# A hybrid decoder layer: the scaling of the attention probabilities goes from VectorE to GpSimd, GpSimd's scalings get a second scalar, and the stores of the normed rows change queues

## What is computed

```python
h = rms_norm(x, norm_attn)
o_sb  = stick_breaking_attend(q, k, v)          # 8 heads of 64
# NSA: 8 query heads of 64 over 2 kv groups, three branches, mixed by sigmoid gates
p   = softmax(s_branch)                         # branch = compressed, selected, window
o_nsa = gates[0]*(p_cmp@v_cmp) + gates[1]*(p_sel@v_sel) + gates[2]*(p_win@v_win)
x = x + concat(rms_norm(o_sb), rms_norm(o_nsa)) @ w_out
h2 = rms_norm(x, norm_ffn)                      # the "normed rows"
# router: top-1 of 4 groups, top-2 of 4 experts in it; gated MLP of the chosen experts
x = x + hier_moe(h2);  y = rms_norm(x, norm_final)
```

## Time and profile before

| | before |
|---|---|
| runs, median (lowest to highest) | 805.37 us (804.71 to 805.73) |
| the profiled execution's own time | 809.19 us |
| its span, first to last instruction | 807.3 us |
| TensorE busy | 734.5 us (91%) |
| VectorE busy | 374.0 us (46%) |
| ScalarE busy | 219.6 us (27%) |
| GpSimd busy | 105.5 us (13%) |
| mean granted TensorE clock | 0.953 |

### The profile page before, as it was taken

The page is one execution under the profiler, slowest core; times in us unless marked ns, Lnnn a source line. Parts: engine busy times, 40 slices in busy tenths (PEclk is TensorE's granted clock), DMA queues, the critical chain, the costliest instruction groups (busy, mean ns, idle before and its releaser), DMA issues.

```text
span 807.3 us, 12441 instructions
## 1 busy us (share of the span) xinstructions
PE 734.5 (91%) x4713; PEld 396.8 (49%) x4713; DVE 374.0 (46%) x804; ACT 219.6 (27%) x561; POOL 105.5 (13%) x111
## 2 busy tenths in 40 slices
PE   4987899997999698999989986789999999999987
PEld 2554456443645454545555553355555554454532
DVE  5521103376130647695995956364144332323146
ACT  1211111020221364667767731001111101110113
POOL 0121000120000470220210211200000000000050
PEclk9999899999999668999999998789999999999999
DMA  9135881647433970000000255889899999999992
GB/s 332 32 94 167 238 312 41 206 124 234 164 130 109 285 288 1 2 3 1 1 28 1 105 180 213 265 269 318 297 400 410 407 405 398 408 401 400 409 384 109
DMA packets 99422, 172.98 MB, mean 214 GB/s; under 512 B 21314, under 2 KB 38562, under 8 KB 99330
## 3 DMA queue, kind: packets, MB, share of 16 engines
q1 hardware_dynamic: 87986, 150.76, 52.7%
q10 hardware_dynamic: 8112, 11.24, 3.8%
q0 software_dynamic: 3264, 10.17, 3.5%
HBM read 152.95 MB, written 21.28 MB: 216 GB/s over the span
## 4 chain that ended last, share of the span: by engine, by line
PE 53%; DVE 9%; issue 5%; ACT 4%; DMA 4%; POOL 0%; ACTq 0%; DVEq 0%; SPq 0%
PE bank L2417 18%; PE bank L2850 5%; PE bank L1820 5%; PE bank L2408 4%; PE bank L2451 4%; PE bank L2832 4%; PE bank L1766 2%; PE bank L1747 2%; PE bank L2541 1%; PE bank L2536 1%; DVE st L1409 1%; DMA work<-h_rows,ids 1%; PE bank L2400 1%; PE bank L2464 1%; PE bank L1658 1%
## 5 line engine op out<-in xcount | busy, mean ns | idle before, releaser
L2850 PE MATMUL bank<-reg 128*128 128x512 f32 (+1 forms) x384 | 168.1, 585 | 1.2 <-DVE reg L2791 0.9
L2417 PE MATMUL bank<-reg,qreg 128*32 128x128 f32 (+2 forms) x848 | 130.4, 389 | 0.8 <-issue 0.8
L2850 PEld LDWEIGHTS bank<-reg 128*128 128x128 f32 x384 | 72.6, 198 | 70.3 <-issue 67.5
L2417 PEld LDWEIGHTS bank<-reg,qreg 128*32 128x32 f32 (+2 forms) x848 | 66.8, 139 | 59.5 <-issue 48.2
L2832 PE MATMUL bank<-cf,reg 128*128 128x128 f32 (+1 forms) x384 | 63.2, 285 | 18.6 <-DVE reg L2782 9.5
L1820 PE MATMUL bank<-reg 128*128 128x512 f32 x128 | 63.8, 622 | 0.4 <-DVE x L1527 0.3
L2832 PEld LDWEIGHTS bank<-cf,reg 128*128 128x128 f32 (+1 forms) x384 | 43.4, 146 | 36.7 <-issue 30.5
L2707 ACT ACTIVATE work<-bank 128x128 f32<-128x128 f32 (+6 forms) x107 | 40.8, 412 | 44.8 <-PE bank L2832 43.9
L2791 DVE COPY work<-bank 128x128 f32<-128x128 f32 (+4 forms) x56 | 23.2, 428 | 54.1 <-PE bank L2832 54.0
L1249 ACT ACTIVATE reg<-bank,st 128x128 f32<-128x128 f32 (+3 forms) x64 | 33.1, 524 | 40.7 <-DVE st L1409 40.6
L1766 PE MATMUL bank<-work,vreg 128*64 128x128 f32 x480 | 38.5, 291 | 2.1 <-DVE work L2791 1.8
(11 more groups left out here) (340 smaller groups left out, 940.1 us busy)
## 6 DMA issues: line engine op xcount, KB each, us to landing
reg<-w_gate SPq DMA_DIRECT2D x12, 2048.0 KB, 20.3
reg<-w_up SPq DMA_DIRECT2D x12, 2048.0 KB, 22.5
reg<-w_down SPq DMA_DIRECT2D x12, 2048.0 KB, 20.2
reg<-w_in SPq DMA_DIRECT2D x16, 512.0 KB, 6.0
expert_rows<-vreg SPq DMA_DIRECT2D x11, 512.0 KB, 5.3
reg<-cache_sb_k SPq DMA_DIRECT2D x16, 256.0 KB, 4.6
reg<-cache_sb_v SPq DMA_DIRECT2D x16, 256.0 KB, 4.8
qreg<-w_up SPq DMA_DIRECT2D x2, 2048.0 KB, 15.9
```

What stands on the lines that cost most here:

```text
L2417: ins = T.matmul(bank[which][rows, at_:at_ + w], rowsT[b][:, k, r0:r0 + n], w_[:, k, h * w:(h + 1) * w], start=(k == 0), stop=(k == KD - 1))
L2850: ins = nc.tensor.matmul(at("m", ("proj", n))[:, 0:w], hT[:, k, i * P:(i + 1) * P], win[:, pos % 2, k, 0:w], start=(k == 0), stop=(k == KD ...
```

## The change

1. Step `share` is split. VectorE only inverts the sums (L1415) and signals `inverse`; GpSimd waits for it and does the two scalings, with the same two scalars, and signals `shared`.
2. GpSimd's one-scalar scalings (`scale_wout`, and the first instruction of `h2`) get a second scalar, a column of ones, so that all of GpSimd's scalings have the two-scalar form.
3. The stores of the normed rows of the sample tile and of tiles 0, 1 and 2 are issued by SP instead of ScalarE. The last tile's is still issued by ScalarE, but its step stands behind `parts`.
4. `expert0_down` becomes four steps: chunks 3, 4 and 2 at its old place, chunk 5 inside the last tile's products (behind the eighth), with the same waits. The list now has SP's stores of tiles 0 and 1 ahead of chunk 3, and tile 2's between chunks 2 and 5.

```diff
@@ ffn_rows
         sg.mark("h2", i)
+        if i != QT - 1:
+            store_rows(i)
+
+    def store_rows(i):
         step("store_h2", i)
         sg.mark("st_h2", i, 16)
@@ share
         step("share", *u)
+        sg.mark("inverse", u)
         sg.mark("shared", u)
@@ after the agenda
-    step("expert0_down")
+    for n in (3, 4, 2):
+        step("chunk", n)
@@ the last tile's products
         product(QT - 1, n)
+        if n == 7:
+            step("chunk", 5)
@@
     route_parts(QT - 1)
+    store_rows(QT - 1)
     route_group(QT - 1)
@@ SP
+        elif kind == "store_h2":
+            i, = key
+            if i == QT - 1:
+                return
+            sg.wait(sp, "h2", i)
+            sp.dma_start(h2_dram[i * P:i * P + ROWS[i], :], h2[0:ROWS[i], :]).then_inc(sg["st_h2"], 16)
@@ GpSimd
+        if kind == "share":
+            i, b, p = key
+            n, w = (i + 1) * P, unit_sums(key)
+            gate = gate_rows(i)[:, b, p, :]
+            if key == nsa_units[0]:
+                sg.wait(pool, "gates", 0)
+            sg.wait(pool, "inverse", key)
+            for e in range(2):
+                prob = prob_of(key, e)[:, 0:n]
+                ins = G.tensor_scalar(prob, prob, w[:, e:e + 1], gate[:, e:e + 1], ALU.mult, ALU.mult)
+            ins.then_inc(sg["shared"], 1)
@@ GpSimd, scale_wout
-            G.tensor_scalar(w_out[:, k0, :], w_out[:, k0, :], gainT[:, k0:k0 + 1], None, ALU.mult
+            G.tensor_scalar(w_out[:, k0, :], w_out[:, k0, :], gainT[:, k0:k0 + 1], c["one"], ALU.mult, ALU.mult
@@ GpSimd, h2
-            G.tensor_scalar(h2[0:r], x[0:r, i, :], small[0:r, 12:13], None, ALU.mult).then_inc(sg["h2"], 1)
+            G.tensor_scalar(h2[0:r], x[0:r, i, :], small[0:r, 12:13], c["one"][0:r], ALU.mult, ALU.mult
+                            ).then_inc(sg["h2"], 1)
@@ VectorE, share
-            link(V.reciprocal(w, w))
-            for e in range(2):
-                prob = prob_of(key, e)[:, 0:n]
-                ins = V.tensor_scalar(prob, prob, w[:, e:e + 1], gate[:, e:e + 1], ALU.mult, ALU.mult)
-            ins.then_inc(sg["shared"], 1)
+            V.reciprocal(w, w).then_inc(sg["inverse"], 1)
@@ ScalarE: its store_h2 step returns at once unless i == QT - 1
@@ SP: the waits and loads of expert0_down, now one step each
+        elif kind == "chunk":
...
+            load_chunk(sp, n, CHUNKS[n][1])
```

More of the change, by code:

```diff
@@ L1137, in gps_more @@
         G = nc.gpsimd
-        if kind == "scale_wout":
+        if kind == "share":
[9 more added lines that the diff above has]
+            ins.then_inc(sg["shared"], 1)
+        elif kind == "scale_wout":
             k0, = key
@@ L1294, in act_more @@
             inverse_rms(small[0:ROWS[i], 12:13], D, "rstd", ("ffn", i))
[L1295 to L1298, removed]
         elif kind == "parts":
@@ L1303, in act_more @@
             nc.scalar.copy(parts[:, 0:r], at("t", ("parts", i))[:, 0:r]).then_inc(sg["t_act"], 1)
+        elif kind == "store_h2":
+            i, = key
+            if i != QT - 1:
+                return
+            sg.wait(act, "h2", i)
+            act.dma_start(h2_dram[i * P:i * P + ROWS[i], :], h2[0:ROWS[i], :]).then_inc(sg["st_h2"], 16)
         elif kind == "slots":
@@ L1410, in dve_more @@
         elif kind == "share":
-            i, b, p = key
-            n, w = (i + 1) * P, unit_sums(key)
-            gate = gate_rows(i)[:, b, p, :]
+            w = unit_sums(key)
             sg.wait(dve, "gb_act", key)
-            link(V.reciprocal(w, w))
-            for e in range(2):
-                prob = prob_of(key, e)[:, 0:n]
-                ins = V.tensor_scalar(prob, prob, w[:, e:e + 1], gate[:, e:e + 1], ALU.mult, ALU.mult)
-            ins.then_inc(sg["shared"], 1)
+            V.reciprocal(w, w).then_inc(sg["inverse"], 1)
         elif kind == "cmp_masks":
@@ L1996, in expert_sync @@
             load_chunk(sp, 1, 0)
[L1997 to L2006, removed]
+        elif kind == "chunk":
+            n, = key
+            if n == 3:
+                sg.wait(sp, "z_full", sb_units[-1])
+            elif n == 4:
+                sg.wait(sp, "t_full", ("probT",) + turned[-1] + (1,))
+            elif n == 2:
+                sg.wait(sp, "pv", turned[-1])
+                sp.wait_ge(sg["st_v"], sg.total["st_v"])
+            else:
+                sg.wait(sp, "m_full", ("wout", QT - 1, 1))
+            load_chunk(sp, n, CHUNKS[n][1])
         elif kind == "experts":
```

## The result

The changed kernel took 801.13 us (median of 7 runs, 799.78 to 806.6), beside 805.73 us before: a ratio of 0.9928, 95% interval 0.9899 to 0.9958. Two later measurements on other chips gave 0.9920 (0.9889 to 0.9951) and 0.9887 (0.9851 to 0.9924). So it is faster, by about 7 us as the mean of the three ratios (0.9912) and 4.6 by the two medians of the first; 12.3 had been forecast. The sign and the range held, the size did not. The profiled execution took 802.79 us with a span of 801.0.

The account below looks back on a forecast made before the run. Attention was taken as mostly TensorE's work, with VectorE late where TensorE stops. Attention 9.5 plus tail 2.8 gave 12.3 us: 796.9 us for the profiled execution, 793.1 for the median, range 787 to 803.

Parts of the forecast that it names:

- The tail: End of the last tile: moved stores free ScalarE's waits in tile 2 (1.6 us) and the last tile (1.2); gain 2.8 us.
- Chunk 3: SP's queue: goes out some 10 us later behind tile 1's normed rows, covered by 40 us until the experts; cost 0.
- The attention: Attention stage, 268 to 475 us: 7.8 - 0.5 + 3.2 - 1.0 = 9.5 us gained.
- of 1.94 and 2.21 all (three shares each): TensorE's two waits for ScalarE's copy of a transpose, with VectorE behind them: both vanish wholly as three shares each leave VectorE.
- of the 2.22 us all: TensorE's wait for VectorE's last product of the compressed shares: all returns, as small operations no longer stand beside GpSimd's slices.
- Of 1.43 all: TensorE's wait for VectorE's addition of an output product: all returns, as two shares of 0.6 to 0.7 us leave VectorE.
- Of the other 9.7 us a third: The rest of TensorE's idle time in the attention: a third returns, 3.2 us.
- the allowance: Attention: 0.5 us taken off for what comes to light behind the four long waits.
- The new waits: Attention, shares and normed rows waiting in GpSimd's queue: 1 us for all new waits, 0 to 4.
- The rival that the two engines hold each other up: Attention: 32 scans meet shares, 14.4 of 32.6 us lost; attention gains 4.7, total 797.9 us; chance 0.17.
- the rivals at 800.6 and 802.6: 800.6: two-scalar form as slow, cover takes it, attention gains 2; 802.6: only the tail gains; chance 0.08 each.
- TensorE as the bound: Attention: TensorE is the bound and its idle time only moves, so only the tail gains, 802.6 us; chance 0.08.

Follow-up runs that it names:

- the stores alone: The kernel before with only the new order of stores and chunks, both scalings untouched: 801.43 us, ratio 0.9919.
- the rows early: The changed kernel with the normed rows of the sample tile and tiles 0 and 1 placed 100 units earlier: 799.86 us, 0.9888; repeat 798.33 us, 0.9873.
- the slices later: The changed kernel with normed rows 100 units earlier and the eight `w_out` slices 30 units later: 795.39 us, ratio 0.9835.
- no scaling at all: The changed kernel with normed rows 100 units earlier and the 64 probability scalings left out: one execution, attention 198.90 us, idle 11.0.
- slices later again: The changed kernel with normed rows 100 units earlier and `w_out` slices 30 units later, measured again on another chip: ratio 0.9889.

## Why the forecast was too large

**The tail**: forecast 2.8, measured 2.7, by the mechanism and at the rows named. Right.

**Chunk 3** went out at 468.88 instead of 457.05 (forecast: 10 us later, no cost), in the run of the stores alone at 455.85; the stretches behind are 296.6 and 295.3 us, within the spread that the clock makes. Nothing of a cost shows.

**VectorE's load** fell as forecast. GpSimd's slices were nearly as forecast (1.19 us for 1.04), its shares dearer by 44% (41.5 us for 28.8). What that cost stands among the new waits below.

**The attention**: forecast 9.5 less idle time, measured 4.1, and 5.8 (17.3 to 11.5) once the rows are early. The step that failed is "of 1.94 and 2.21 all (three shares each)", 4.15 of the 9.5 us: these waits were credited to VectorE's load and don't depend on it. They were 1.94 and 2.21 before, 1.95 and 2.22 with the stores alone, 1.94 and 2.22 with VectorE scaling beside shorter GpSimd instructions, 1.94 and 2.21 with the rows early, 1.95 and 2.22 with the slices later, and 1.94 and 2.22 with no scaling at all. (In the changed kernel the hold-ups stand just ahead of them, and they vary: 1.94 and 0.71, none and 2.28, 1.13 and 0.91.) The forecast took VectorE for late there, "at the end of a run of work without idle time". But that run itself begins with a wait for TensorE. The kernel before, VectorE and TensorE in order of time:

```profile
409.93 1.22 DVE L1409 TENSOR_REDUCE st<-bank 128x2 f32<-128x1024 f32 x1 [0.35 <-PE bank L1749]
...
412.49 0.18 PE L1863 MATMUL bank<-onehot,cb 128*128 128x16 bf16 x1
...
413.95 0.15 DVE L1591 TENSOR_TENSOR rt<-rt 128x1 f32<-128x1 f32 x1
```

The same places with the rows early, where VectorE has no scaling, all engines in order of time:

```profile
402.54 1.22 DVE L1438 TENSOR_REDUCE st<-bank 128x2 f32<-128x1024 f32 x1 [0.98 <-PE bank L1772]
...
405.10 0.18 PE L1886 MATMUL bank<-onehot,cb 128*128 128x16 bf16 x1
...
406.56 0.15 DVE L1614 TENSOR_TENSOR rt<-rt 128x1 f32<-128x1 f32 x1
...
406.75 0.30 ACT L1338 ACTIVATE rt<-rt 128x4 f32<-128x4 f32 x1 [1.51 <-DVE rt L1614]
...
407.14 1.00 ACT L1250 ACTIVATE work<-bank 128x1024 f32<-128x1024 f32 x1
...
411.12 0.59 ACT L2732 ACTIVATE work<-bank 128x512 f32<-128x512 f32 x1
...
411.86 1.09 PE L2857 MATMUL bank<-cf,x 128*128 128x128 f32 x4 [2.21 <-ACT work L2732]
```

Without the scalings VectorE only waits longer ahead of the run, 0.98 us instead of 0.35. From its maximum to the router's last small step it takes 4.02 us in both. From TensorE's product of the ranks to the end of its wait are 6.75 us before (412.49 to 419.24) and 6.76 after. So this is a loop: TensorE's products release VectorE's run, that releases ScalarE, and that TensorE. No share lies in it: the two that VectorE did at 402.05 and 408.57 stand ahead of its wait for TensorE, and the one at 415.33 comes behind the router's last small step, with its transposes at 423.93. The idle time in front of VectorE's run, in the profile before, would have told it. What sets the length of the loop stays open: with ScalarE's exponentials out of it, TensorE still stopped for 1.8 and 2.3 us. A harder test came by chance: in the run without scaling three of VectorE's scans were held for 2.77, 3.05 and 3.32 us instead of 0.67, 0.93 and 1.20, and no kernel has less idle time.

The other terms, first profile of the changed kernel against the one before: "of the 2.22 us all" gave 1.7 of it, by the hold-ups that it named, though a late landing would have given the same. "Of 1.43 all" gave half, 0.7. "Of the other 9.7 us a third" was too low: without the four waits and the new ones the idle time fell from 9.5 to 4.4 us, and to 4.5 with the rows early, where the forecast had 3.2 less. So with the rows early the attention misses 9.5 by 3.7: 4.15 of the two loops, 1.3 of the first two waits and 0.5 of the new ones too much, and 0.5 (the allowance) and 1.8 (the others) too little.

**The new waits** are the second step that failed: forecast 1.0 us, found 1.5 on GpSimd's shares in tile 0 and 3.8 behind the two hold-ups, 5.3 in all. Moving the rows removed the 3.8 and gave 1.7 of idle time back, as the second loop's wait grew in their place. The forecast had seen that GpSimd "stops running ahead" and that the normed rows would stand behind shares, and asked only how long the next share would wait, not whom the moved 2.35 us instruction would hold up on VectorE. The rival that the two engines hold each other up was nearest in its time (797.9; the three measurements give 0.9912 of 805.4, 798.3), though not at the scans that it named: they took 1.22 and 1.20 us for 512 columns in the changed kernel and 1.23 and 1.20 with the rows early, and only two of the 32, of 256 columns, took 0.2 us longer (0.89 and 0.90 for 0.68). The long ones of the kernel before, 1.81 us for 384 columns and 2.07 for 512, are gone. By the first measurement's median, 801.13, the rivals at 800.6 and 802.6 are as near.

**TensorE as the bound** got 0.08 and deserved more. That is the case for tiles 2 and 3, where the wait for VectorE "by name" is a loop that TensorE itself starts. That the time stayed inside the forecast's range says nothing for the mechanism: the range reached down to where only the tail gains.

## What to carry to other kernels

Before a wait is credited to an engine's load, follow that engine's run back to its start: if it begins with idle time ended by the engine that waits, the wait is the length of a loop, and work taken off in front of it or behind it changed nothing here. When work moves onto an engine that had run ahead, look at where its other long instructions now land, on which small operations of the engine that shares memory access with it, and whether they can be placed elsewhere. And where one profile shows a long wait beside a transfer's landing, take a second profile before counting on it.

## What the runs showed beside the question

**A second scalar makes GpSimd's scaling faster.** 128x1024 took 2.84 to 2.88 us with one scalar and 1.19 with two, the second being a column of ones.

**Which VectorE operations are held up.** Beside GpSimd's product, VectorE's scaling of 8 columns from SBUF to SBUF took 1.6 us longer, but the reduction of 256 columns of SBUF just ahead of it ran in its usual 0.42 us while that product was running (353.52).

**The clock goes with most of the spread of executions.** The six executions of slices later again run from 794.50 us at a mean clock of 0.958 to 803.04 at 0.947, nearly in its order. From 15 to 26 us into the attention TensorE was granted 0.50 (1.2 GHz) in the first profile of the changed kernel and 0.95 in the third. The busy share had been the same, 12.8 of 15 us ahead of it in both:

```profile
285.50:296.50 11.00, 10.31 (x67) 5.64 (x71) 4.32 (x15) 5.38 (x22) 5.39 (x9) 0.50 1.00 396
```

```profile
284.80:295.80 11.00, 10.19 (x104) 5.72 (x104) 5.87 (x16) 7.97 (x34) 7.13 (x10) 0.95 1.01 402
```

TensorE did 104 products in the third and 67 in the first, and the attention was 4.0 us shorter with 0.5 us less idle time. The stretch "behind" is 295 to 297 us or 299 to 301, and this goes with the clock of its first 60 us, not with the kernel: in the profiles it was 0.93 to 0.95 for the short ones and 0.82 to 0.91 for the long ones. The same program twice (slices later, and again):

```profile
498.60:558.60 60.00, 57.98 (x537) 33.58 (x539) 29.60 (x80) 6.45 (x14) 6.13 (x7) 0.95 0.90 307
```

```profile
497.50:557.50 60.00, 56.12 (x397) 30.66 (x401) 27.40 (x76) 4.83 (x10) 5.33 (x6) 0.87 0.84 281
```

At 0.95 the rest took 294.8 us, at 0.87 301.0. Why the stores alone measured 0.9919 with a tail 3 us shorter stays open in part. Its executions had a high clock, 0.956 to 0.958; the median of the five at 0.956 is 802.1 us, and of the six of the kernel before, in the same measurement, at 0.955 to 0.957 it is 807.4. These 5.3 us are near what its profile shows, 3.0 of tail and 2.5 of idle time, of which 1.6 lie in tile 0, where `w_out` landed late. The landing of its first piece varied from 4.5 to 10.5 us behind the first score product over the fourteen profiles, with the same transfers ahead of it, and none of the moved stores comes before it; whether the unprofiled executions had it late too, no run here shows. So in device time the two halves of the change, the stores and the scalings, are not told apart: that the scalings gave anything beyond the stores rests on idle times alone.
